# Two-block transformer on one core: eight parts of the ada weights move from the ring of dense weights to the first expert buffer

## The reference

```python
def first_block(...):
    ada = silu(c) @ w_ada + b_ada                    # w_ada 1024 x 6144
    sh_m, sc_m, g_m, sh_f, sc_f, g_f = split(ada, 6)
    h = modulate(rmsnorm(x), sh_m, sc_m)
    cq, ckv, k_rope, fq, fk, fv, f_logit, g_mla, g_fox = split(h @ w_in)
    q = rmsnorm(cq) @ w_uq ; kv = rmsnorm(ckv) @ w_ukv          # 8 heads each
    y = sigmoid(g_mla) * (mla_attention @ w_o_mla) + sigmoid(g_fox) * (fox_attention @ w_o_fox)
    x = x + g_m * (y @ w_out)
    x = x + g_f * conv_ffn(modulate(rmsnorm(x), sh_f, sc_f))
def second_block(...):
    h = x + (short_conv | diff_attention) @ w_out_2
    h = h + moe(h)        # 32 experts, 2 per token, w_gate, w_up 1024 x 512, w_down 512 x 1024
```

## Time and profile before

| what | value |
|---|---|
| three runs | 1050.13, 1052.65, 1058.01 us, median 1052.65 |
| the profiled execution | 1051.05 us, its span 1049.3 us |
| PE busy | 975.0 us, 93% of the span |
| DVE, ACT, POOL busy | 452.0, 376.0, 27.1 us |
| HBM read | 307.31 MB, of them 201 MB expert weights |
| mean granted clock of TensorE | 0.98 of full speed |

### The profile page before, as it was taken

One profiled execution on the slowest core, in us unless ns is written; L12 is line 12 of the kernel. 1 busy time (PEld: TensorE's weight loads), 2 busy tenths in 40 slices (PEclk: granted clock), 3 DMA queues, 4 the chain that ended last, 5 costly groups with the idle time before them and its releaser, 6 DMA issues.

```text
span 1049.3 us, 15094 instructions
## 1 busy us (share of the span) xinstructions
PE 975.0 (93%) x6239; PEld 670.1 (64%) x6239; DVE 452.0 (43%) x837; ACT 376.0 (36%) x709; POOL 27.1 (3%) x60
## 2 busy tenths in 40 slices
PE   4799899999899999999898899999999999998987
PEld 1697667889799999987788644344444444343433
DVE  2443476657588558758666511112121211101113
ACT  2344355554466446554453431111111111121210
POOL 1000000000000000002201000000000000000000
PEclk9899999999899999999898999999999999999999
DMA  9672954284275455354644769999999999999996
GB/s 388 260 289 93 345 232 161 82 319 162 82 287 195 161 203 199 121 220 168 239 176 161 310 276 428 429 426 427 428 429 427 427 427 428 427 428 428 426 427 253
DMA packets 23254, 309.35 MB, mean 295 GB/s; under 512 B 2576, under 2 KB 3088, under 8 KB 3984
## 3 DMA queue, kind: packets, MB, share of 16 engines
q1 hardware_dynamic: 23040, 307.32, 72.1%
q10 hardware_dynamic: 144, 1.05, 0.3%
HBM read 307.31 MB, written 1.05 MB: 294 GB/s over the span
## 4 chain that ended last, share of the span: by engine, by line
PE 36%; DMA 11%; DVE 2%; issue 1%; ACT 0%; DVEq 0%
PE ps L949 35%; DMA ring<-experts 4%; DMA work<-experts 4%; DMA slot<-experts 4%; PE ps L1484 1%; PE ps L1426 0%; DVE wb L2021 0%; PE ps L1294 0%; ACT pickT L925 0%; DVE wa L2012 0%; DVE wl L1556 0%; ACT wc L927 0%; DVE wb L2043 0%; DVE aL L2108 0%; ACT wh L562 0%
## 5 line engine op out<-in xcount | busy, mean ns | idle before, releaser
L1556 DVE TENSOR_TENSOR wl<-ring,wh 128x1024 fp32r<-128x1024 f32 (+4 forms) x156 | 184.0, 1191 | 122.5 <-ACT wh L562 122.1
L562 ACT ACTIVATE wh<-ring 128x1024 fp32r<-128x1024 f32 (+4 forms) x156 | 159.5, 1032 | 164.0 <-PE ps L949 126.9
L949 PE MATMUL ps<-hH,wh 128*128 128x256 f32 x704 | 201.3, 286 | 6.6 <-ACT wb L648 2.1
L949 PE MATMUL ps<-hL,wh 128*128 128x256 f32 x704 | 198.8, 282 | 0.0
L949 PE MATMUL ps<-hH,wl 128*128 128x256 f32 x704 | 198.5, 282 | 0.0
L949 PEld LDWEIGHTS ps<-hH,wh 128*128 128x128 f32 x704 | 134.4, 191 | 10.9 <-issue 5.6
L949 PEld LDWEIGHTS ps<-hL,wh 128*128 128x128 f32 x704 | 134.3, 191 | 0.0
L949 PEld LDWEIGHTS ps<-hH,wl 128*128 128x128 f32 x704 | 134.1, 191 | 0.0
L2213 DVE SCALAR_TENSOR_TENSOR wc<-wc,w_slot,ps 128x512 f32<-128x512 f32 x16 | 11.9, 747 | 219.4 <-PE ps L949 219.4
L949 PE MATMUL ps<-aH,wh 128*128 128x256 f32 x304 | 86.9, 286 | 1.6 <-DVE aL L1776 1.1
L949 PE MATMUL ps<-aL,wh 128*128 128x256 f32 x304 | 86.1, 283 | 0.0
(11 more groups left out here) (342 smaller groups left out, 1384.0 us busy)
## 6 DMA issues: line engine op xcount, KB each, us to landing
ring<-dense SPq DMA_DIRECT2D x42, 2048.0 KB, 8.1
ring<-experts SPq DMA_DIRECT2D x28, 2048.0 KB, 28.4
slot<-experts SPq DMA_DIRECT2D x28, 2048.0 KB, 29.4
work<-experts SPq DMA_DIRECT2D x20, 2048.0 KB, 28.5
early<-experts SPq DMA_DIRECT2D x10, 2048.0 KB, 26.4
wb<-experts SPq DMA_DIRECT2D x9, 2048.0 KB, 25.8
ring<-dense SPq DMA_DIRECT2D x5, 1024.0 KB, 4.8
work<-dense SPq DMA_DIRECT2D x2, 2048.0 KB, 24.3
```

The costliest lines, as they stand in the source:

```text
L562: nc.scalar.activation(wh[:, c % CHUNKS, 0:n], src, ACT.Copy).then_inc(S("chunk_high"), 1)
L949: return nc.tensor.matmul(o_, l, r, start=start, stop=stop, skip_group_check=True)
L1556: V.tensor_tensor(wl[:, c % CHUNKS, 0:n], src, wh[:, c % CHUNKS, 0:n].bitcast(F32), ALU.subtract)\
```

## The change

The four parts of the second third of ada (ada10 to ada13) and the four of the last third (ada20 to ada23) get a slot of their own, number 7, which is the tensor `early`. Nothing is computed differently, and the order of the list is the same, so SP issues the same loads in the same order. What each load waits for is different:

```diff
+EARLY = 7
-    ada_item(1, 0)
+    ada_item(1, 0, EARLY)
     in_item("fk", 2)
-    ada_item(1, 1)
+    ada_item(1, 1, EARLY)
     in_item("fv", 0)
-    ada_item(1, 2)
+    ada_item(1, 2, EARLY)
...
-    ada_item(1, 3)
+    ada_item(1, 3, EARLY)
     half_item("ukv", 1, "w_ukv", 2, 512, 0)
     for i, acc in enumerate((2, 0, 0, 0)):
         in_item(f"g{i}", acc)
-        ada_item(2, i)
+        ada_item(2, i, EARLY)
...
-            return {3: slot3[:], 4: work[:, 0:SLOT], 5: work[:, SLOT:2 * SLOT], 6: slot6[:]}[i]
+            return {EARLY: early[:], 3: slot3[:], 4: work[:, 0:SLOT], 5: work[:, SLOT:2 * SLOT], 6: slot6[:]}[i]
...
-            if i in (1, 2):
+            if i == 0:
+                name = f"slot{EARLY}_loaded"
+            elif i in (1, 2):
...
                 if it["name"] == "up4":
+                    sp.wait_ge(S("ada_used"), IT["ada23"]["ada"])
                     load_unit(0)
```

## The result

The changed kernel takes 1078.36 us (median of four runs, 1074.09 to 1083.66) against 1051.39 us for the one before: ratio 1.024, with a 95% interval of 1.0205 to 1.0275. The forecast was 1066.7 with a range up to 1074. The direction was right, and so was what the change does to the queue; the size was not. Medians and intervals leave out one execution of 1068.29 us, of the first experiment, that fell in a slower state. The profiled execution is the slowest of the four, 1083.66 us with a span of 1081.9, so 32.6 us of span stand against those 27.

A forecast was written before the change was run, and what follows sets the result against it. PE was taken as the bound, busy 975.0 of 1049.3 us, with loads also at their bound in the expert stage. Terms -0.2 + 0.4 + 4.8 + 4.1 + 1.0 + 4 = +14.1 us gave 1066.7 us, range 1056 to 1074.

The forecast's parts named there:

- The queue: SP's in-order load queue: each dense load behind an ada part lands later by one transfer, 4.8 us.
- fv: Load after ada11: lands at 81.2 instead of 76.96 us, first chunk ready at 83.5; PE loses 1.9 us.
- clock term: Slower clock after the idle times at g2 and g3: 2 us each, +4 in all (0 to 7).
- g0 and g1: g0's 2.13 us of idle time covers the earlier shift, sum -0.2; g1's second chunk is late, +0.4 (0 to 1).
- the sign that was named for it: In the profile after, there should be no wait of 2 us ahead of g0.
- g2, g3, om0: Attention: dense loads land behind ada21, ada22 and ada23, costing +4.8, +4.1 and +1.0 us (the last 0 to 3.5).
- The end: Expert stage: keeps its length; each microsecond lost in the dense stage moves the end one for one.
- From om1 on: Later loads come earlier than before and nobody waited for them: no effect.
- The full price: Half-speed clock for 7 us after both stalls, +6.8, and fv's stall uncovered at g0, +2: 1071.5 us; chance 0.16.
- No loss of clock: Same stalls at full clock, +10.1: 1062.8 us; chance 0.17.
- not slower: ACT's chunk lead absorbs late loads; PE wins 2.13 us ahead of g0 and 0.49 at 153.06: 1050.0 us; chance 0.06.
- half of it: Paired transfers overlap, so g2 and g3 are late by only 2 us each: +5, 1057.5 us; chance 0.09.

The follow-up runs named there:

- the first experiment: Changed kernel with only the second third (ada10 to ada13) sharing the early buffer, ada20 to ada23 in the ring as before: 1058.67 us, ratio 1.0028.
- This half by itself: Changed kernel with only ada20 to ada23 sharing the early buffer, ada10 to ada13 in the ring as before: 1068.49 us, ratio 1.0138.

## Why the prediction was wrong

- **The queue.** "The dense load, which ACT waits for, lands later by the transfer of one ada part": right. g2 landed 13.1 us after its issue against 7.9 before, and reversing the order undid all of the loss.
- **fv.** "PE loses 1.9 us" is the step that failed. The stall was 2.8 us: from the end of ada10 to ACT's start at fv it took 13.7 us where the step has 12.9. That is a small miss, but the term left out the clock. The prediction has a clock term for the two long stalls alone and gives no reason for none here, though its own show that 2.1 us of idle time left the clock at 1.00 once and had it at 0.72 once; and it took the whole shift as covered by the idle time ahead of g0. The stretch cost 16.9 us in one profiled execution, 9.1 in the second and 9.2 in that with the second third alone, of which the lateness is under 3. With PE's gap filled it was 3.1 at a clock of 1.00.
- **g0 and g1.** The stretch gave back 1.5 us in the first profile and 1.4 in the second, where the steps said 1.7. But the sign that was named for it, no wait of 2 us ahead of g0, is there in one of the two only: 0.68 us in the first and 1.98 in the second. In the kernel before and in the first profile PE lost 1.7 us on the way to g0 to 3.4 us of low clock, in the second it did not. Late as PE was, g0's load was late with it: it goes out 9.0 us after ada12's start in both, when uq1 has been split, and lands 9.4 us later, where the step took 7.9.
- **g2, g3, om0.** 5.92 us of idle time forecast as 5.3, 4.11 as 4.1, and om0's stretch +1.2 for +1.0. The clock behind g2 was a mis-sized term: down for 14 us of which some 4.7 reached the end, where I took 2 with an upper bound of 3.4; behind g3 it cost 1.6. My bound came from the one stretch of 7 us in the earlier trace rows, of which the last 4.5 are one run of a projection's matmuls of 256 columns. Behind the stall at g2 such a run, the gate's chunk, starts only 8 us later, at 180.3, and the clock came back 4.5 us into it. This half by itself measured +15.5 against 13.9.
- **The end.** The dense stage's shift went to the end one for one, to within 2 us. From om1 on nothing changed, as forecast.
- **The rivals.** "The full price", 1071.5 us, named the right cause with too low a ceiling, and not at fv, where it counts the stall alone. "No loss of clock" is ruled out by the low clock behind the stalls, "not slower" and "half of it" by the stalls themselves. The Trainium skill ("TensorE: Matmul & The Clock Gate", section HAM oscillation) describes a kernel in which each wait for a load, of some 3 to 5 us, throttles PE again. The profiles agree behind g2 and g3, and show the same for a shorter wait at fv, where 2.7 to 2.8 us were followed by it in three profiles out of four. I had cited that section and set one row against it that disagreed, and priced the spell by another stage.

## What to carry over

In a single in-order load queue, a buffer that is refilled only when it is empty holds back every load behind it: put the loads that somebody waits for ahead of the refill, and read a new buffer's value from the queue's order, not from the number of slots. A stall on PE has to be priced with the work behind it: if that work is short or thin matmuls, some 3 us of idle time can cost 9 or 17 us, as at fv here. And where one execution of several is much slower, compare two profiles of the same kernel before believing the length of anything in one.

## What had not been expected of the hardware

After an idle time of 2.7 to 2.8 us the granted clock was at 0.50 for 31, 14 and 14 us in three executions, and didn't fall in a fourth in which the matmuls behind it all had 512 columns. In two of the three it fell only 1.6 to 1.7 us after PE was at work again. With an idle time of 10 us ahead of the same fv it was down for 31 us in all, 25 of them in fv, and for 10 in all, under 5 of them in fv, without its matmuls of 8 columns. And 24 useless matmuls in a gap of 3 us made the changed kernel 6 to 9 us faster.
